# Projecting values before queries and keys in the first group, and preparing the first attention pair inside the last projection section

## The reference, cut to what matters

```python
hp = rms_norm(xp, norm_mix[0])            # x / rms(x) * gain
z = hp @ w_in                             # group a: q, k, v and forget logits; group b: q, k, v (512 columns each)
qa = rms_norm(heads(z[..., 0:D_A]), g_qa) # per head of 64, queries and keys alike
ka = rms_norm(heads(z[..., D_A:2*D_A]), g_ka)
va = heads(z[..., 2*D_A:3*D_A])           # values: no norm
logf = log_sigmoid(z[..., 3*D_A:ob] + b_f)
# group b: the same, and rotary on the first 16 of 64 columns of q and k
oa = fox_attention(qa, ka, va, cumsum(logf), ...)   # bias c_q - c_k, causal softmax
ob = dilated_mixture(qb, kb, vb)                    # three dilations, causal softmax
x += concat(oa, ob) @ w_out
```

## Time and profile before

| what | value |
|---|---|
| runs | 2630.19 us median of 3 (2628.05 to 2633.6) |
| profiled execution | 2626.38 us, its span 2624.3 us |
| PE busy | 2556.8 us, 97% |
| DVE, POOL, ACT busy | 1133.9, 1101.6, 550.1 us |
| slice 1 of 40 of the span (66 us each) | PE 7 tenths busy; all others 8 or 9 |

### The profile page before, as it was taken

The page is one execution under the profiler, slowest core; times in us unless marked ns, Lnnn a source line. Parts: engine busy times, 40 slices in busy tenths (PEclk is TensorE's granted clock), DMA queues, the critical chain, the costliest instruction groups (busy, mean ns, idle before and its releaser), DMA issues.

```text
span 2624.3 us, 42745 instructions
## 1 busy us (share of the span) xinstructions
PE 2556.8 (97%) x16331; PEld 2344.0 (89%) x16331; DVE 1133.9 (43%) x2258; ACT 550.1 (21%) x1266; POOL 1101.6 (42%) x702
## 2 busy tenths in 40 slices
PE   7999989999999999999999999899999999999999
PEld 5777756666899999999999987899999999999999
DVE  6636536667344333333333360553733333333333
ACT  5201136666322000000000051322300000000001
POOL 4234115566665444333344262435654443333440
PEclk9999999999999999999999999999999999999999
DMA  5223148767312111111111111111121111111111
GB/s 158 70 80 91 60 129 247 217 203 211 96 34 73 49 43 45 44 44 48 48 48 48 33 49 32 49 33 49 33 65 48 44 43 45 43 48 48 48 32 65
DMA packets 218459, 189.83 MB, mean 72 GB/s; under 512 B 29443, under 2 KB 171523, under 8 KB 217956
## 3 DMA queue, kind: packets, MB, share of 16 engines
q1 hardware_dynamic: 200996, 161.89, 21.2%
q10 hardware_dynamic: 17344, 26.35, 2.8%
HBM read 171.19 MB, written 17.01 MB: 72 GB/s over the span
## 4 chain that ended last, share of the span: by engine, by line
PE 69%; DVE 2%; POOL 2%; ACT 1%; issue 1%; ACTq 0%; POOLq 0%; PEldq 0%; DVEq 0%
PE ps L536 63%; PE ps L566 1%; PE ps L568 1%; PE ps L567 1%; ACT ps L2079 1%; POOL Xl L509 1%; POOL Wl L392 1%; POOL Wh L389 1%; DVE hs L479 0%; PE ps L2042 0%; POOL acc_sq L450 0%; PE ps L1265 0%; PE ps L1293 0%; PE ps L2211 0%; DVE VM_EARLY L2163 0%
## 5 line engine op out<-in xcount | busy, mean ns | idle before, releaser
L536 PE MATMUL ps<-Xh,Wh 128*128 128x256 f32 (+2 forms) x2712 | 872.6, 322 | 9.7 <-PE ps L536 3.3
L536 PE MATMUL ps<-Xl,Wh 128*128 128x256 f32 (+2 forms) x2712 | 867.4, 320 | 0.0
L536 PE MATMUL ps<-Xh,Wl 128*128 128x256 f32 (+2 forms) x2712 | 866.4, 319 | 0.0
L389 POOL TENSOR_TENSOR Wh<-raw,zeros 128x1024 fp32r<-128x1024 f32 x178 | 353.9, 1988 | 1072.5 <-PE ps L536 782.4
L536 PEld LDWEIGHTS ps<-Xh,Wh 128*128 128x128 f32 x2712 | 510.3, 188 | 15.6 <-issue 8.8
L536 PEld LDWEIGHTS ps<-Xh,Wl 128*128 128x128 f32 x2712 | 510.9, 188 | 0.0
L536 PEld LDWEIGHTS ps<-Xl,Wh 128*128 128x128 f32 x2712 | 510.3, 188 | 0.7
L392 POOL TENSOR_TENSOR Wl<-raw,Wh 128x1024 fp32r<-128x1024 f32 x178 | 440.9, 2477 | 14.0
L1839 DVE TENSOR_TENSOR Hl<-hf,Hh 128x392 fp32r<-128x392 f32 (+1 forms) x132 | 181.8, 1377 | 464.8 <-ACT Hh L1775 464.8
L536 PE MATMUL ps<-Hh,Wh 128*128 128x392 f32 (+2 forms) x1056 | 340.7, 323 | 1.2 <-DVE xT L1848 1.2
L536 PE MATMUL ps<-Hl,Wh 128*128 128x392 f32 (+2 forms) x1056 | 338.1, 320 | 0.0
(11 more groups left out here) (251 smaller groups left out, 2485.9 us busy)
## 6 DMA issues: line engine op xcount, KB each, us to landing
raw<-in_w_gate_up SPq DMA_DIRECT2D x88, 512.0 KB, 3.8
raw<-in_w_down SPq DMA_DIRECT2D x44, 512.0 KB, 3.5
kring<-in_cache_a_k SPq DMA_DIRECT2D x64, 256.0 KB, 3.6
ring<-in_cache_a_v SPq DMA_DIRECT2D x64, 256.0 KB, 3.1
raw<-in_w_in_even SPq DMA_DIRECT2D x20, 512.0 KB, 4.1
raw<-in_w_in_c SPq DMA_DIRECT2D x16, 512.0 KB, 3.9
xs<-in_x_prompt SPq DMA_DIRECT2D x8, 512.0 KB, 8.5
q_prompt<-zt ACTq DMA_DIRECT2D x16, 256.0 KB, 2.0
```

What stands on the lines that cost most here:

```text
L389: pool.tensor_tensor(h[:, :], r[:, :], zeros[:, :].to_broadcast([P, 1024]), ALU.add).then_inc(split_high, 1)
L536: ins = nc.tensor.matmul(out, w, x, start=(j == 0), stop=(j == len(pairs) - 1))
```

## The change

1. The sections of group 0 run in the order values, queries, keys (`SECTIONS`); group 1 keeps queries, keys, values. The 1/rms of each tile is made on its own: ACT's root tile by tile (`input_std`), DVE's reciprocal ahead of the tile's scaling.
2. In group 1's last section (values) the four query and key tiles of the first pair are loaded (`att_early_sp`), transposed behind tiles 4 to 7 (`early_pair`), and copied; the first bias is loaded too. For this the attention buffers take places in the weight buffers that this section doesn't use.
3. `forget_pe` moves behind the first unit's scores and uses banks 5 to 7; `forget_dve` moves into attention's step u = -1; the mask is made by `attention_masks` right behind the last section; first values are loaded right behind the constants.
4. In attention `reciprocals(u + 1)` stands ahead of `log_sum` and `biased(u + 2, 1)`.
5. The output projection's second weight unit onwards is loaded only after the last `biased`, since its buffer now holds `QT`.
6. The loop over i = 1 is written out on PE, ACT and DVE.

```diff
+        SECTIONS = [(2, 0, 1), (0, 1, 2)]
+        def input_std(act, tt):
+            act.wait_ge(x_squared, tt + 1)
+            act.activation(msx[:, tt:tt + 1], ssx[:, tt:tt + 1], ACT.Sqrt, bias=eps[:, 0:1], scale=1.0 / D).then_inc(x_std, 1)
+        def early_pair(i, c, pos):
+            return pos - 4 if (i, c) == (1, 2) and 4 <= pos < 8 else None
...
+                        if early_pair(i, c, tt) is not None:
+                            transpose_qk(pe, 0, early_pair(i, c, tt), 3 + early_pair(i, c, tt))
...
-                        if is_first(i) and c == 0 and tt == TT - 1:
-                            dve.wait_ge(x_std, 1)
-                            dve.reciprocal(rstd[:, :], msx[:, :]).then_inc(x_rstd, 1)
+                        if is_first(i) and c == 0:
+                            for t in inputs_behind(tt):
+                                input_scale(dve, t)
+                            dve.wait_ge(x_std, tt + 1)
+                            dve.reciprocal(rstd[:, tt:tt + 1], msx[:, tt:tt + 1]).then_inc(x_rstd, 1)
...
+        def att_early_sp(sp):
+            sp.wait_ge(split_done, 25)
+            for j in range(NZ):
+                sp.wait_ge(z_out[j], 16 * (NZT + 2 * TT) // NZ)
+            for n in range(2):
+                load_qk(sp, n)
+            sp.wait_ge(z_ps, NZT + 2 * TT)
+            sp.wait_ge(c_out, 16)
+            for part in range(3):
+                load_first_bias(sp, part)
+            for n in range(2, 4):
+                load_qk(sp, n)
...
+        def attention_masks(dve):
+            dve.wait_ge(z_ps, 2 * NZT)
+            dve.tensor_copy(ident16[:, :], ident[:, :])
+            dve.tensor_scalar(above16[:, :], tri[:, :], -1.0, -NEG, ALU.add, ALU.mult).then_inc(lp_zero, 1)
...
-            for g in range(4):
-                transpose_qk(0, g, g)
-            pe.wait_ge(lp_zero, 2)
             for u in range(-2, NUNIT):
...
+                if u == -2:
+                    forget_pe(pe)
...
                 biased(u + 2, 0)
+                if u == -1:
+                    forget_dve(dve)
                 if u >= 0:
                     after_window(u)
...
+                reciprocals(u + 1)
                 tiles = log_tiles(u)
                 for sample, tile in tiles[0:1]:
                     log_sum(sample, tile)
                 biased(u + 2, 1)
-                reciprocals(u + 1)
...
-            load_narrow(sp, BASE_OUT, a["w_out_even"][0], 8)
+            load_narrow(sp, BASE_OUT, a["w_out_even"][0], 0, 1)
+            sp.wait_ge(s_biased, 2 * chunk_base[NUNIT])
+            load_narrow(sp, BASE_OUT, a["w_out_even"][0], 1, 8)
```

More of the change, by code:

```diff
@@ L337, in load_wide, with load_narrow @@
                 load_unit(sp, base + j, j + (base % SPL if isinstance(base, int) else 0), rows(w, 2 * j, 2, col, DH), 2)
-        def load_narrow(sp, base, w, count):
-            for m in range(count):
+        def load_narrow(sp, base, w, first, end):
+            for m in range(first, end):
                 load_unit(sp, base + m, base + m, rows(w, 0, KT, m * P, P), KT)
@@ L556, in build, with sections @@
         NZT = 3 * TT
+        SECTIONS = [(2, 0, 1), (0, 1, 2)]
+        def sections(i):
+            return SECTIONS[0 if is_first(i) else 1]
         def wide_part(tt, bank, s0, k, stacked):
@@ L711, in in_pe @@
                 input_transpose(pe, tt)
-            peeled_loop(pe, 2, step)
+            for i in range(2):
+                step(i)
             pe.wait_ge(z_ps, 2 * NZT)
@@ L739, in in_store, with qk_tile @@
             act.dma_start(dst, zt[q % NZ][0:r, :]).then_inc(z_out[q % NZ], 16)
+        def qk_tile(i, c, pos):
+            return i * 2 * TT + [x for x in sections(i) if x < 2].index(sections(i)[c]) * TT + pos
         def sample_low(act, i, c, q):
@@ L778, in step @@
                             input_high(act, t)
-                        if c < 2:
+                        if sections(i)[c] < 2:
                             act.wait_ge(z_sum, n + 1)
@@ L810, in in_act @@
             input_square(act, 2)
-            peeled_loop(act, 2, step)
+            for tt in range(3):
+                input_std(act, tt)
+            for i in range(2):
+                step(i)
         def in_dve(dve):
@@ L880, in in_dve @@
             input_low(dve, 1)
-            peeled_loop(dve, 2, step)
+            for i in range(2):
+                step(i)
         lg, lg_a = sem("lg"), sem("lg_a")
@@ L1003, in att_begin_sp @@
                 sp.wait_ge(z_out[j], 16 * 2 * NZT // NZ)
-            for n in range(3):
-                load_qk(sp, n)
             sp.dma_start(hmask[:], a["c_hmask"]).then_inc(att_const_in, 16)
             sp.dma_start(dbias[:, :, SLOTS - 3:LOG, :], a["c_dbias"]).then_inc(att_const_in, 16)
-            sp.wait_ge(c_out, 16)
         def own_sp(sp):
@@ L1155, in att_sp @@
                     load_key(0, j)
-                for part in range(3):
-                    load_pair_values(sp, 0, part)
                 own_sp(sp)
@@ L1391, in copy_sums @@
                 act.activation(Rs[u % 2][:, :], ps[:, 4 + y % 2, 0:P], ACT.Copy).then_inc(pt_out, 1)
-            def copy_queries_keys(it, g, bank):
-                cols = slice((6 - 2 * g) * P, (8 - 2 * g) * P)
-                act.wait_ge(qk_ps, 4 * it + g + 1)
-                act.activation(QT[:, cols], ps[:, bank, 0:2 * P], ACT.Copy)
-                act.activation(KTr[:, cols], ps[:, bank, 2 * P:4 * P], ACT.Copy).then_inc(qk_act, 1)
-            for g in (0, 2):
-                copy_queries_keys(0, g, g)
-            act.wait_ge(lp_zero, 2)
             def loads(it, j):
```

189 lines of the change are left out of this document (103 added, 86 removed).

## The result

| kernel | median us (runs) | ratio to before, 95% interval |
|---|---|---|
| before | 2630.65 (2628.05 to 2633.6) | 1 |
| after | 2611.16 (2606.86 to 2612.55) | 0.9923 [0.9908, 0.9939] |

The forecast was 2612.3 us. The profiled execution of after has a span of 2609.9 us, 14.4 us under that of before; the medians stand 19.5 us apart, since the profiled execution of before was 4.3 us under its median and that of after 0.7 us over.

The account below looks back on a forecast made before the run. The prediction took PE as the bound, busy 2556.8 of 2624.3 us, leaving 67.5 us idle. Terms 8.8 - 3.4 + 11.5 + 1.0 = 17.9 us off 2630.2 gave 2612.3 us, with an 8-in-10 range of 2602 to 2621.

Parts of the forecast that it names:

- Values first: First section: DVE no longer late, so the second section starts at 70.98 instead of 79.76; 8.8 us won.
- Full work comes back: Group 0's keys to group 1's queries: POOL's splits delay DVE, PE waits 1.85 us, then half clock; 3.4 us lost, bounds 0 to 6.8.
- First pair early: Way into attention: second unit's weights 14.5 us behind the last product instead of 28.2, less 2.2 for transposes; 11.5 us won.
- SP has nothing behind them that anyone waits for: Last projection section: the first pair's early loads cost nothing, as nothing queued behind them on SP is awaited.
- third rival: Attention's start: first units held by page sums, exponential and sample loads, clock may fall; 5 won rather than 11.5, 2618.8 us; chance 0.09.
- Reciprocals first: Attention: PE's waits for the reciprocal mostly become waits for the exponential; 1 us of 8.5 won.
- nearly all of the 8.5 us: Attention: the share of PE's reciprocal waits said to stand at the eight pair starts and turn into exponential waits.
- second rival: Attention: `biased` starts earlier, the exponential follows and the full 8.5 us of reciprocal waits go; 2604.8 us; chance 0.10.
- Output units later: Output projection: later weight unit loads cost nothing, with some 4 us of cover; without it, up to 4.1 us.
- both boundaries: Projection: the stall also comes between group 0's queries and keys, 3.4 us more; 2615.7 us; chance 0.14.
- slower: Attention: the moved reciprocal holds back `biased` and the next exponential in every unit; 2638.9 us at 0.4 us each; chance 0.03.
- nothing: Whole kernel: first section held by arrival of inputs, attention by its loads, so no gain; 2630 us; chance 0.02.

Follow-up runs that it names:

- e4: Kernel after, with the second group's in-projection writing to four PSUM banks in turn instead of three: 2603.99 us, 0.9906 of before.
- e6: Kernel after, with the second pair's first query and key tile loaded early and four banks in the second group's projection: 2596.15 us, 0.9878 of before.
- e11: Kernel before, with only VectorE's reciprocal moved ahead of the first log sum and second half of the biased scores: 2625.49 us, 0.9983 of before.
- e12: Kernel after, unchanged, measured once more: 2610.72 us, 0.9920 of before; profiled span 2617.3 us.
- e10: Kernel after, with group 0's sections again queries, keys, values and VectorE's input scaling behind the sample rows' sum: 2616.57 us, 0.9950 of before.
- e9: e6, with the page sums' products ahead of the first scores and VectorE's operations on them ahead of the first biased scores: 2602.16 us, 0.9893 of before.
- e8: e6, with the first pair's 16 transposes and their copies behind the last section again, loads still early: 2604.06 us, 0.9900 of before.
- e1: Kernel after, with the second pair's first query and key tile loaded ahead of the last section's end: 2606.64 us, 0.9910 of before.
- e7: e6, with VectorE's reciprocal put back behind the second half of the biased scores: 2603.11 us, 0.9896 of before.
- e13: e6, unchanged, measured once more beside e12: 2597.69 us, 0.9877 of before.
- e5: Kernel after, with GpSimd splitting only 256 of 1024 columns of group 1's key and value weights (numbers wrong): 2603.68 us, 0.9902 of before.

## Why the prediction was right, and where it was not

The time was right to 1.1 us and the mechanisms of all four parts are there, but that closeness is luck: the sum came out by errors that cancel.

*Values first (8.8 won, bounds 6.0 to 9.5).* Right. Between executions with the same clock at the start, before and e4, the forget gates' mark comes 9.5 us earlier (94.85, 85.33); in e6 the second section's first product stands at 71.05, forecast 70.98. The profile of after shows only 7.9, since its clock fell at 20 to 25 us, which it does in e11 too, where nothing was changed there.

*Full work comes back (3.4 lost).* Right in place, number and cause: one new wait, between group 0's keys and group 1's queries, none between queries and keys of group 0. (The forecast's heading puts it in the third section; its sign of being right and the trace put it in the fourth, 208.14.) The size was low: the wait is 3.13 us and not 1.85. By the way from the forget gates' mark to the first scores, both boundaries cost 6.8 us in after and 9.9 in e12 (249.8 in e4, 259.6 in e12), the old one alone 3.8 in e10 (253.6): 3.0 to 6.1 for the new one.

*First pair early (11.5 won, bounds 7 to 13.5).* Right. 13.3 us instead of 28.2, less 2.2 for the transposes: 12.7. It was forecast as 14.5; the page sums kept PE waiting for 0.83 us and nothing else stuck out. e9 shows what their place is worth, about 5 us, and e8 that the transposes must be early for the sake of two buffers, which I had not seen.

*What failed.* The step "SP has nothing behind them that anyone waits for", which put the queue's part in the sum at nothing. I looked at the loads that move, and at who waits for what is queued behind them, but not at the loads that stay. The second pair's first tile kept its place, 11.2 us behind the first issue after the section's end (346.51 to 357.71). Before, attention came to it some 29 us after the last product; once the start had shrunk to 14 the queue itself was the bound: 6.4 to 7.3 us (e1, e4 and e6). The third rival came nearest to this, with a transfer that holds attention's start, but named the wrong ones.

*Reciprocals first (1 won, bounds -4 to 8.5).* The mechanism, a wait that becomes one for the exponential, is right at the pair starts. The mis-sized term is "nearly all of the 8.5 us". Six of the twelve waits stand ahead of a pair's first weights, 6.8 us in all (403.37, 444.28, 484.40, 525.82, 566.38 and 650.18); in after five of these places wait for the exponential, 4.7 us in all. The other six made 1.7 us, of which the last, 0.35, is left. So 8.5 us became 4.7 and 0.6, with 1.1 more for `Lm` (1.0 before, 2.1 after). Measured: 5.4 to 7.0 us (e7) and 5 us [2.1 to 6.8] (e11) by the medians, 5.4 by e7's trace, 0.9 in the stretch by e11's. So about 5 us, between my value and the second rival's, and not sure to better than 2 us; what e11's median won outside its stretch was not traced.

*Output units later (nothing).* Right: no wait for a weight unit between 660 and 690 us in after, e6 to e9, e12 and e13.

*Sum.* Forecast 8.8 - 3.4 + 11.5 + 1.0 = 17.9. Measured about 9 - 4.5 + 12.7 + 5 - 7.3 = 15, with the spread that the clock gives. That agrees with the 14.4 us between the two profiles; the medians say 19.5, with an interval of 16 to 24, and the few microseconds between are not accounted for by any part. The loss that I missed was half made up by a part that I had valued at a fifth. The rivals "both boundaries", "slower" and "nothing" found no support.

## What to carry to other kernels

When a change takes many microseconds out of a stretch, go through every transfer that this stretch needs, above all those that the change doesn't touch: their place in the queue was measured against the old length. A wait on a buffer can be an engine's passing hold-up by another engine; a bank more of lead (e4) removed it here without touching the cause. And when the longest wait of a kind differs between executions of one kernel, follow it back to a transfer before taking its releaser for the cause.

## What the runs showed of the hardware

- A VectorE operation with two inputs in SBUF doesn't merely slow down beside GpSimd's: 0.29 us become 2.37, and it ends within 0.2 us of the end of GpSimd's instruction (e5), while a sum with one input keeps its 0.67. This fits what the Trainium skill, SBUF — State Buffer, "Who interferes with whom", says of a lock for a whole instruction.
- Whether the granted clock falls behind a wait of about 2 us is not settled by the wait's length. Behind PE's wait near 19.3 us the mean clock in 20 to 25 us was 1.00 in five profiles (waits of 2.17, 1.79, 1.71, 2.17, 2.17 us) and 0.66 to 0.78 in nine (1.91 to 2.18 us), which costs up to 1.7 us. Two profiles of one kernel (after and e12, 2609.9 and 2617.3 us) differ by 7 us though the clock fell there in both: 3.0 us of it by the clock behind the two waits of the projection, 3.4 by waits in attention and what follows them.
